# Two transformer blocks on one core: the opening transfers in K-tile order with the qk stage split tile by tile, and the last down product's second token tile in three pieces

## What is computed

```python
h = rmsnorm(x, norm_mix_g)
proj = h @ w_in                      # first columns: lru_x, lru_gate, then m_qk
...
h = rms_norm(x, pre_ffn_g)
f = jnp.square(jax.nn.relu(h @ w_ff1)) @ w_ff2
x = x + rms_norm(f, post_ffn_g)      # the kernel's output
```

## Time and profile before

| | us |
|---|---|
| median of 3 runs (749.52 to 749.61) | 749.52 |
| the profiled execution: its time | 749.77 |
| its span in the trace | 748.0 |
| PE busy in it | 740.5 (99%) |
| DVE busy | 523.8 (70%) |
| ACT busy | 402.5 (54%) |

### The profile page before, as it was taken

The page is one execution under the profiler, slowest core; times in us unless marked ns, Lnnn a source line. Parts: engine busy times, 40 slices in busy tenths (PEclk is TensorE's granted clock), DMA queues, the critical chain, the costliest instruction groups (busy, mean ns, idle before and its releaser), DMA issues.

```text
span 748.0 us, 10384 instructions
## 1 busy us (share of the span) xinstructions
PE 740.5 (99%) x4280; PEld 648.8 (87%) x4280; DVE 523.8 (70%) x612; ACT 402.5 (54%) x509; POOL 49.7 (7%) x71
## 2 busy tenths in 40 slices
PE   9999999999999999999999999999999999999996
PEld 9988888889988888888899898789988988888885
DVE  6788946885766666656779998785758655556564
ACT  6678378544545545444653685673647443454442
POOL 0200002120000000000230200030003000000000
PEclk9999999999999999999999999999999999999999
DMA  9866365555565556666466536365065466555431
GB/s 337 280 224 225 137 237 210 171 171 168 176 219 169 170 171 204 215 203 209 154 218 205 165 117 225 116 235 165 21 212 166 162 221 225 172 199 188 162 123 57
DMA packets 74239, 138.42 MB, mean 185 GB/s; under 512 B 3916, under 2 KB 28368, under 8 KB 74064
## 3 DMA queue, kind: packets, MB, share of 16 engines
q1 hardware_dynamic: 72336, 132.69, 52.9%
q10 hardware_dynamic: 1856, 5.06, 1.9%
HBM read 136.69 MB, written 1.05 MB: 184 GB/s over the span
## 4 chain that ended last, share of the span: by engine, by line
PE 97%; DVE 2%; issue 0%; ACT 0%; DVEq 0%; ACTq 0%
PE wide L2074 70%; PE bank L2074 25%; PE bank L2198 2%; DVE low L1318 0%; DVE arena L1581 0%; ACT arena L723 0%; DVE act_hl L1415 0%; DVE xn L1809 0%; DVE x L1819 0%; DVE arena L1641 0%; DVE arena L1637 0%; DVE hid_l L1646 0%; DVE arena L1643 0%; DVE arena L1627 0%; DVEq L263 0%
## 5 line engine op out<-in xcount | busy, mean ns | idle before, releaser
L1318 DVE TENSOR_TENSOR low<-raw,high 128x2048 fp32r<-128x2048 f32 (+1 forms) x118 | 267.0, 2279 | 106.2 <-ACT high L723 101.5
L723 ACT ACTIVATE high<-raw 128x2048 fp32r<-128x2048 f32 (+3 forms) x134 | 234.7, 1770 | 122.8 <-PE wide L2074 95.9
L2074 PE MATMUL wide<-act_hl,high 128*128 128x256 f32 (+1 forms) x1184 | 241.3, 327 | 0.0
L2074 PEld LDWEIGHTS wide<-act_hl,high 128*128 128x128 f32 x1184 | 198.9, 191 | 18.3 <-issue 0.2
L2074 PE MATMUL wide<-high,act_hl 128*128 128x512 f32 x528 | 170.1, 394 | 0.5 <-DVE arena L1581 0.2
L2074 PE MATMUL wide<-act_hl,low 128*128 128x256 f32 x832 | 161.2, 284 | 0.0
L2074 PEld LDWEIGHTS wide<-act_hl,low 128*128 128x128 f32 x832 | 128.6, 192 | 2.8 <-DVE low L1366 0.2
L2074 PEld LDWEIGHTS wide<-high,act_hl 128*128 128x128 f32 x528 | 99.1, 188 | 23.3 <-issue 1.7
L2074 PE MATMUL wide<-low,act_hl 128*128 128x512 f32 x264 | 103.0, 390 | 0.0
L2074 PE MATMUL bank<-high,hid_l 128*128 128x512 f32 x216 | 84.4, 391 | 0.3 <-DVE hid_l L1646 0.3
L2074 PE MATMUL bank<-low,hid_h 128*128 128x512 f32 x216 | 84.2, 390 | 0.0
(11 more groups left out here) (215 smaller groups left out, 681.1 us busy)
## 6 DMA issues: line engine op xcount, KB each, us to landing
raw<-in_w_ff_dram SPq DMA_DIRECT2D x32, 1024.0 KB, 5.3
raw<-in_w_in_dram SPq DMA_DIRECT2D x27, 1024.0 KB, 5.3
raw<-in_w_ffn_in_dram SPq DMA_DIRECT2D x44, 512.0 KB, 4.9
raw<-in_w_ffn_out_dram SPq DMA_DIRECT2D x11, 1024.0 KB, 6.5
raw<-in_w_xkv_dram SPq DMA_DIRECT2D x8, 1024.0 KB, 5.0
raw<-in_w_o_dram SPq DMA_DIRECT2D x4, 1024.0 KB, 5.1
raw<-in_w_out_dram SPq DMA_DIRECT2D x4, 1024.0 KB, 5.0
raw<-in_w_xq_dram SPq DMA_DIRECT2D x4, 1024.0 KB, 5.2
```

The lines of the kernel that those rows point to most:

```text
L723: return act.activation(dst, src, func, **k)
L1318: tt(part(low, g), part(raw, g), f32(part(high, g)), SUB).then_inc(sem.low_by_dve, 1)
L2074: return pe.matmul(dst, lhs, rhs, start=start, stop=stop, skip_group_check=loose)
```

## The change

Four parts, all at the two ends of the program.

1. **Order of the first transfers.** The second half of K tile 0's weights is issued by ACT instead of SP. On SP each x_t tile now goes right ahead of its own weight tile; before, x_t came in pairs. `vec` (75 KB of columns) moves from ACT's queue to SP's, behind `x`.
2. **FINE becomes 4.** The second qk group too is brought, copied and subtracted in four K tiles.
3. **`rep_made` moves** from ahead of K tile 5 of the qk stage to ahead of K tile 6.
4. **The tail.** Token tile 1 is made in three pieces: the left half of bank 7 (256 columns), bank 6 (512), the right half of bank 7 (256). Ahead of the third piece PE waits until DVE has read the first (`zg`). `post_acc` has three squares, products and additions for that tile, and its first store is issued by ACT, the other two by SP.

```diff
-        FINE = len(chunks["lru"]) + 1
+        FINE = len(chunks["lru"]) + len(chunks["qk"])
+        LAST_SPANS = (NB, T), (0, NB), (NB + T, T)
+        FIRST_OUT = 2 * 2 * TT + 2 + 1
...
-                if g == FINE + 1:
+                if g == FINE:
                     sp.dma_start(x[:, :, :], w["x"].rearrange("(t p) d -> p t d", p=P)).then_inc(sem.x_in, 16)
-                if g == FINE + 1:
+                if g == FINE:
+                    sp.dma_start(vec[:, :], w["vecs"]).then_inc(sem.vec_in, 16)
...
-                            sp.dma_start(tile[:, 0, T:NB], src[row:row + P, c + T:c + NB]).then_inc(first_in[0], 16)
                             continue
+                        if 2 <= g * n + k < KD:
+                            kt = g * n + k
+                            sp.dma_start(x_t[:, kt:kt + 1, :], w["x_t"][:, kt - 1:kt, :]).then_inc(first_in[kt], 16)
                         sp.dma_start(tile[:, k, :], src[row + k * P:row + (k + 1) * P, c:c + cw])\
-                          .then_inc(first_in[g * n + k], 16)
-                        if g < 2 and k % 2 and g * n + k + 1 < KD:
-                            k0 = g * n + k + 1
-                            sp.dma_start(x_t[:, k0:k0 + 2, :], w["x_t"][:, k0 - 1:k0 + 1, :]).then_inc(first_in[k0], 16)
+                          .then_inc(first_in[(g * n + k) % 12], 16)
...
+            for i, (t, a, size) in enumerate(((0, 0, NB), (0, NB, NB), (1, 0, NB), (1, NB + T, T))):
+                sp.wait_ge(sem.x_ready, X_READY_END - 2 * TT + (1, 2, 4, 5)[i])
+                sp.dma_start(out[t * P:(t + 1) * P, a:a + size], x[:, t, a:a + size]).then_inc(sem.stored, 16)
...
                 act.dma_start(first_x[:, :], w["first_x"]).then_inc(sem.first_x_in, 16)
+                (src, row, n, d, c, cw), = groups[0][0]
+                act.dma_start(part(raw, 0)[:, 0, T:NB], src[row:row + P, c + T:c + NB]).then_inc(first_in[0], 16)
                 act.dma_start(x_t[:, 1:2, :], w["x_t"][:, 0:1, :]).then_inc(sem.x_t_in, 16)
-                act.dma_start(vec[:, :], w["vecs"]).then_inc(sem.vec_in, 16)
...
             def first_high(kt):
-                act.wait_ge(first_in[kt], 32 if 2 <= kt < KD and kt % 2 == 0 else 16)
+                act.wait_ge(first_in[kt % 12], first_count(kt))
+                if kt == 12:
+                    act.wait_ge(sem.w_used, 1)
...
+                act.wait_ge(sem.x_ready, X_READY_END - 1)
+                act.dma_start(out[P:2 * P, NB:NB + T], x[:, 1, NB:NB + T]).then_inc(sem.stored, 16)
...
-                    for ns in ((0, 1),) if t == 0 else ((0,), (1,)):
+                    for piece in range(1 if t == 0 else 3):
+                        spans = LAST_SPANS[piece:piece + 1] if t else ((0, NB), (NB, NB))
+                        if piece == 2:
+                            pe.wait_ge(sem.zg, FIRST_OUT)
...
-            products("qk", "C", at={5: rep_made})
+            products("qk", "C", at={6: rep_made})
```

More of the change, by code:

```diff
@@ L300, in two_blocks @@
         sums = sb("sums", [P, TT, 2])
+        third_sum = sb("third_sum", [P, 1])
         var = sb("var", [P, 32])
@@ L422, in two_blocks @@
         sem = Semaphores(lambda name: ctx.enter_context(nc.semaphore(name)))
-        FINE = len(chunks["lru"]) + 1
-        first_in = [ctx.enter_context(nc.semaphore(f"first_in{k}")) for k in range(4 * FINE)]
+        FINE = len(chunks["lru"]) + len(chunks["qk"])
+        first_in = [ctx.enter_context(nc.semaphore(f"first_in{k}")) for k in range(12)]
         raw_in = [ctx.enter_context(nc.semaphore(f"raw_in{s}")) for s in range(RAW)]
@@ L429, in first, with first_count @@
             return part(tiles, kt // 4)[:, kt % 4, :]
+        def first_count(kt):
+            mine = 32 if 2 <= kt % 12 < KD else 16
+            return mine if kt < 12 else mine + 16
         def arrived(g):
@@ L557, in _ @@
                       .then_inc(raw_in[g % RAW], 16)
[L559 to L564, removed]
+            for i, (t, a, size) in enumerate(((0, 0, NB), (0, NB, NB), (1, 0, NB), (1, NB + T, T))):
+                sp.wait_ge(sem.x_ready, X_READY_END - 2 * TT + (1, 2, 4, 5)[i])
+                sp.dma_start(out[t * P:(t + 1) * P, a:a + size], x[:, t, a:a + size]).then_inc(sem.stored, 16)
+            sp.wait_ge(sem.stored, 80)
         @block.gpsimd
@@ L847, in first_split @@
                     act.wait_ge(sem.x_t_in, 16)
-                elif kt % 2 == 0:
+                else:
                     act.wait_ge(first_in[kt], 32)
@@ L1095, in post_acc @@
                     act.wait_ge(sem.ffn_scale, t + 1)
-                    for c in range(2):
-                        if c == 0:
+                    for i, (a, size) in enumerate(LAST_SPANS if t else ((0, NB), (NB, NB))):
+                        if i < 2 and i <= t:
                             act.wait_ge(sem.tile0_used, me.seen("tile0_used"))
@@ L1100, in post_acc @@
                             act.wait_ge(sem.w_used, me.used)
-                        f(post_junk[:, t, c * NB:(c + 1) * NB], bank[4 + 2 * t + c][:, :], ACT.Square,
-                          scale=inv[:, TT + t:TT + t + 1], accum_out=sums[:, t, c:c + 1]).then_inc(sem.post_sum, 1)
+                        f(post_junk[:, t, a:a + size], bank[4 + 2 * t + a // NB][:, a % NB:a % NB + size], ACT.Square,
+                          scale=inv[:, TT + t:TT + t + 1], accum_out=last_sums[t][i]).then_inc(sem.post_sum, 1)
                     k = 2 * (POST + 2) + t
-                    act.wait_ge(sem.post_sum, 8 + 2 * t + 2)
+                    act.wait_ge(sem.post_sum, 8 + (2, 5)[t])
                     act.wait_ge(sem.left_sum, t + 1)
-                    f(rstd[:, k:k + 1], sums[:, t, 1:2], ACT.Sqrt, bias=var[:, k:k + 1]).then_inc(sem.post_sd, 1)
+                    f(rstd[:, k:k + 1], last_sums[t][-1], ACT.Sqrt, bias=var[:, k:k + 1]).then_inc(sem.post_sd, 1)
+                act.wait_ge(sem.x_ready, X_READY_END - 1)
+                act.dma_start(out[P:2 * P, NB:NB + T], x[:, 1, NB:NB + T]).then_inc(sem.stored, 16)
             def x_exp(i):
@@ L1365, in first_low @@
                 dve.wait_ge(sem.first_high, kt + 1)
+                if kt == 12:
+                    dve.wait_ge(sem.w_used, 1)
                 tt(first(low, kt), first(raw, kt), f32(first(high, kt)), SUB)\
@@ L1803, in post_acc @@
                     k = 2 * (POST + 2) + t
-                    for c in range(2):
+                    spans = LAST_SPANS if t else ((0, NB), (NB, NB))
+                    for i, (a, size) in enumerate(spans):
                         dve.wait_ge(sem.post_sum, me.seen("post_sum"))
-                        if c == 0 and t == 0:
+                        if i == 0 and t == 0:
                             dve.wait_ge(sem.row_in, me.seen("row_in", 16))
[L1808 to L1811, removed]
+                        stt(xn[:, t, a:a + size], bank[4 + 2 * t + a // NB][:, a % NB:a % NB + size], inv[:, t:t + 1],
+                            row_g[:, a:a + size], MUL, MUL).then_inc(sem.zg, 1)
+                        if t == 0 and i == 0:
                             ts(var[:, k:k + 1], sums[:, t, 0:1], EPS, None, ADD).then_inc(sem.left_sum, 1)
-                    dve.wait_ge(sem.zg, me.seen("zg", 2))
+                        elif t == 1 and i == 1:
+                            ts(var[:, k:k + 1], sums[:, t, 0:1], sums[:, t, 1:2], EPS, ADD, ADD).then_inc(sem.left_sum, 1)
+                    dve.wait_ge(sem.zg, me.seen("zg", len(spans)))
                     dve.wait_ge(sem.post_sd, t + 1)
@@ L1816, in post_acc @@
                     dve.wait_ge(sem.dve_step, me.step())
-                    for c in range(2):
-                        cut = slice(c * NB, (c + 1) * NB)
-                        stt(x[:, t, cut], xn[:, t, cut], rstd[:, k:k + 1], x[:, t, cut], MUL, ADD)\
+                    for a, size in spans:
+                        stt(x[:, t, a:a + size], xn[:, t, a:a + size], rstd[:, k:k + 1], x[:, t, a:a + size], MUL, ADD)\
                             .then_inc(sem.x_ready, 1)
@@ L2165, in last_down @@
                                 in_h, in_l = (half[:, kt, t * P:(t + 1) * P] for half in hidden_of(c, False))
[L2166 to L2170, removed]
+                                for a, size in spans:
+                                    cut = slice(a, a + size)
+                                    ins = mm3(bank[4 + 2 * t + a // NB][:, a % NB:a % NB + size], in_h, in_l,
+                                              wh[:, j, cut], wl[:, j, cut], False, kt == 3)
+                            if t == 1 and piece == 2:
                                 ins.then_inc(sem.w_used, 1)
-                        if t == 0 or ns == (0,):
+                        if t == 0 or piece < 2:
                             ins.then_inc(sem.tile0_used, 1)
```

1 line of the change is left out of this document (added).

## The result

The changed kernel takes 752.32 us (median of 6 runs, 751.95 to 752.99) against 749.51 (6 runs, 749.16 to 749.61): a ratio of 1.0037, 95% interval 1.0027 to 1.0047. It is slower by 2.8 us; the forecast was 751.75. The profiled execution took 752.46 with a span of 750.7, which is 2.7 more than before, and the two ends share it: 1.18 up to the start of the last product's second token tile, 1.52 behind that.

What follows compares the result with a forecast made beforehand. PE was taken as the bound, 97% of the chain, with DVE close behind. Head +0.8 and tail +1.45 on the profiled 749.77 make 752.0; the median being 0.25 lower, the forecast was 751.75 us, range 750.0 to 753.2.

Steps and rivals of the forecast that it cites:

- (a): Likeliest case: PE waits both at the vo stage and at the tail's third piece, giving 751.75 us; chance 0.62.
- The unbroken DVE row bounds vo: Head: DVE works without gaps from `rep` to group 6's `low`, which PE needs at vo; slack 0.15 us.
- (b): Rival at the head: group 6's `low` is no bound at vo, so head -0.6, total 750.4 us; chance 0.12.
- The spreading one K tile later, less the gain of 0.45: 25.81: Head: the row factor's spreading starts at 24.82 + 1.44 - 0.45 = 25.81 us, making `rep` 0.83 later.
- 1.25 less the gain: Head: rule for the loss at vo; gains of 0.2 to 0.6 in the first transfers give +1.05 to +0.65 us.
- The gain of 0.45: Head, first products: PE loses 0.45 us to late K tile 2 weights, and the new transfer order wins it back.
- The second half of K tile 0 leaves ACT when SP would have sent it: Head, first transfers: issuing this half from ACT, which still issues three transfers, costs nothing.
- The counting of bytes ahead of K tile 2: Head: 203 KB less queued ahead of K tile 2's weights brings them 0.53 us earlier at 395 GB/s.
- The tail: +1.93 at the last matmul, then -0.35, -0.27, +0.14, in all +1.45: PE's wait delays the last matmul 1.93; square -0.35, last `xn` -0.27, additions +0.14; bounds 1.1 to 1.8 us.
- (c): Rival at the tail: DVE reaches its first product before the additions, short wait; tail -0.2, total 750.1 us; chance 0.10.
- (d): Rival: PE's clock falls during the tail's wait, the last 12 matmuls take +1.4 us, total 753.2; chance 0.05.
- (e): Rival at the head: split transfers run slower, at 280 GB/s `x` lands 2.2 us later, total 753.2; chance 0.06.

Runs made afterwards that it cites:

- e3: The changed kernel with the row factor's spreading (`rep_made`) back ahead of K tile 5 of qk: 750.94 us, ratio 1.0019.
- e4: The changed kernel with the row factor's spreading (`rep_made`) moved on to ahead of K tile 7 of qk: 755.06 us, ratio 1.0068.
- e9: The changed kernel with DVE's `low` of group 6 moved ahead of `scaled_in` for qk: 751.86 us, ratio 1.0029.
- e1: The kernel before with only the tail's four edits, everything at the head as before: 750.88 us, ratio 1.0017.
- e2: The kernel before with only the head's edits, everything at the tail as before: 751.31 us, ratio 1.0023.
- e8: The changed kernel with the second qk group whole again (FINE 3), `x` and `vec` still behind it: 752.25 us, ratio 1.0038.
- e5: The changed kernel with the second half of K tile 0's weights issued by SP again, not ACT: 751.94 us, ratio 1.003.
- e7: The changed kernel with spreading ahead of K tile 5, K tile 0's half on SP, first tail piece's square and product before token tile 0's root: 749.6 us.
- e11: The changed kernel with three repairs (spreading, SP half, tail order), group 6's `low` earlier, and `x` brought and summed ahead of the second qk group: 749.29 us.

## Why the prediction was right, point by point

**Both waits, rival by rival.** The likeliest case (a) came. In the order of the prediction's steps:

- *The unbroken DVE row bounds vo.* Right: the row behind `rep` kept its length, and moving the spreading alone (e3, e4) or the `low` alone (e9) moves vo's start. Case (b) is out.
- *Distance from the spreading to `rep`, 0.73; PE's four passes without a wait, 0.45.* Measured 0.65 (26.37 to 27.02) and 0.36 (26.37 to 26.73), a little less in both.
- *The spreading one K tile later, less the gain of 0.45: 25.81.* This is the step that was mis-sized: it was at 26.37. The rule under it, 1.25 less the gain, holds: with the gain at -0.1 it gives 1.35, and 1.30 was measured instead of +0.8, outside the +0.65 to +1.05 that were given for the head. The gain of 0.45 was read from one execution of the kernel before. In e1, with the same first transfers, K tile 3's second matmul is at 10.02 instead of 10.54, with nothing left to win; in the seven traces with the new order and the half on ACT it is between 10.03 and 11.20.
- *"The second half of K tile 0 leaves ACT when SP would have sent it ...: nothing."* This is the term that failed. Two transfers now stood ahead of x_t tile 1 on ACT's queue, while SP's queue already had K tile 1's 256 KB of weights under way. K tile 0's second half let ACT go on at 5.21 (before 4.16, both halves in one row), and the x_t tile behind it at 6.41 instead of 4.77. The counting of bytes ahead of K tile 2 fits, for K tiles 2 and 3 flowed; but the half that left SP's queue now came ahead of K tile 1's x_t. The Trainium skill's page "DMA: Bandwidth & Descriptors", section "Issuing engines are not separate DMA queues", says that transfers issued by different engines run interleaved on the same 16 engines, and that issuing on several saves only issue time. The trace agrees: x_t was issued at 1.72 and took 4.67 to land, where the same tile, with no half ahead of it on ACT's queue, took 3.2 before.
- *The tail: +1.93 at the last matmul, then -0.35, -0.27, +0.14, in all +1.45.* Measured +1.90 at the last matmul (7.11 against 5.21 from the first of the tile), then -0.38 in all behind it, together 1.52. The square gave 0.3, the product 0.26, the additions cost 0.12, and the store with its issue 0.1. Case (c) is out.
- *(d), the clock.* It did not fall in either wait: the granted clock is 1.00 in the window of the tail's hole. It did in e4, after 2.76 us instead of 1.3. The single slowest runs of e2 (754.03) and e9 (753.84) list a mean clock of 0.996 where the others of these versions have at least 0.998; they were not traced, so whether the clock fell there stays open.
- *(e), slower split transfers.* Out: 402 GB/s in the window where the pieces move (395 before) and 333 in the next (280 before), `x` is summed from 21.0 instead of 21.4, and e8 has the same time with the group whole. The Trainium skill's rule that the prediction cites (page "DMA: Bandwidth & Descriptors", section Bandwidth) asks for 1 MiB or more a transfer; the trace does not agree for transfers queued one behind the other, by the same 402 GB/s.

**The sum.** +0.8 and +1.45 were forecast, +1.30 and +1.52 were measured at the two places, and 0.12 of the first was given back between the vo stage and the tail (1.30 late at 36.93, 1.18 late at 737.90). That is 2.7 in the span instead of 2.25 (2.8 between the medians), and 752.32 instead of 751.75, inside the likeliest case's own range, though near its upper end of 752.4. That the head's extra half microsecond comes from the first queue is shown by the chain of this one trace. For the medians it is not shown: the start of K tile 1 moves by more than that from execution to execution, and e5's 0.4 points the same way but is not beyond its interval.

## What to carry to other kernels

Moving a step on the engine that is never idle moves everything that hangs on its result by the same amount: follow that result through the in-order lists of the other engines to where the first engine next needs them, and look at the slack there (0.15 us here, against 1.44 of delay). A piece of work that may start only when another engine has read the bank is worth nothing if that reading stands behind older work in the other engine's list; split the list together with the tile. When a repair gives the expected gain locally but not in the time, as e7 and e11, look for the next place where the waits reappear before trying a third repair. A transfer that is brought forward pushes back whatever frees the next buffer: in e11 that cost, 25 us later, what it had won. And one trace is one sample: at the head two executions of the same instructions differed by 0.77 us, more than most of the terms in the sum.

## What was unexpected in the hardware

- PE stood 1.32 us and 1.37 us with the granted clock at 1.00 afterwards; after 2.76 us (e4) it went on at full pace for 1.2 us and then fell to 1.2 GHz for 3.4 us, 0.43 a matmul of 512 columns instead of 0.23. In that execution a wait of twice the length cost three times as much.
- A 128 KB transfer on the second queue, behind another of 128 KB, landed after 4.67 us while the first queue moved 256 KB tiles; with only 132 KB ahead of it on its queue it took 3.2. Over all thirteen traces it was 4.1 to 5.2 against 3.1 to 3.2. The start of K tile 1 scattered over 1.2 us among the seven executions that used that queue so, and over 0.5 among the four of the new order that did not.
- The window from 10.5 to 18.0 us, in which four transfers of 256 KB move in place of one of 1 MB, ran at 402 GB/s, against 395 before.
